# Eight of 24 modulation chunks multiplied on VectorE instead of TensorE

## The chip, the cores and the metric

One Trainium2 chip, one of its cores. The metric is the device time of one execution in microseconds; the kernel before was run three times (2601.99, 2604.31 and 2606.24 us, median 2604.31). One more execution was profiled, and all rows of the trace are from that one. [...]

## What is computed

Two blocks on 256 tokens of width 2048, in float32. The first block has an even and an odd attention layer and attends to a memory; the second has a recurrent (LRU) layer and a differential attention layer on the tokens and, in its first layer, on a context of 256 tokens. Every layer of the second block is modulated: shift, scale and gate come from a vector `c` (for the tokens) and a vector `c_ctx` (for the context), each multiplied with a matrix of 2048 x 6144.

```python
def second_block(x, c, ctx, c_ctx, mod_w, mod_b, ...):
    sc, scc = jax.nn.silu(c), jax.nn.silu(c_ctx)
    for i in range(DEPTH):                      # DEPTH = 2
        need_ctx_out = i < DEPTH - 1
        shift, scale, gate = jnp.split(sc @ mod_w[i] + mod_b[i], 3, axis=-1)
        cshift, cscale, cgate = jnp.split(scc @ mod_w[i] + mod_b[i], 3, axis=-1)
        h_lat = rms_norm_2(x, norm_g[i]) * (1.0 + scale[:, None]) + shift[:, None]
        h_ctx = rms_norm_2(ctx, norm_g[i]) * (1.0 + cscale) + cshift
        ...
        x = x + gate[:, None] * y_lat
        if need_ctx_out:
            ctx = ctx + cgate * y_ctx
```

The modulation needs nothing of the first block. Its two matrices are 100 MB of the kernel's 425 MB of loads. The gate of the context in the last layer (`cgate` for i = 1) is never used.

## The kernel before

**Weights.** All weights pass through a ring of 8 slots in SBUF (`ring`, RA). A unit of the ring is two k-tiles of 128 rows by 512 columns, 0.524 MB. SP issues one load for each unit, in the order of the list `RING`, and ahead of each it waits until TensorE has used the unit eight places before (`unit` in the sync program, `s_wused`). For a product in nearly full float32, ScalarE rounds each unit to `ring_hi` (`hi`, L1316; four buffers), VectorE subtracts that from the unit into `ring_lo` (`lo`, L1770), and TensorE does three products of each tile, hi x hi, hi x lo and lo x hi (`multiply`, L716): 12 matmuls a unit.

**Modulation.** The 24 chunks of 512 columns (12 for each of the two matrices, `MOD_CHUNK`) are "mod" units, 8 to a chunk, 192 in all. They aren't split; TensorE multiplies them as they landed, in float32, with the columns of `cond_t` (CS) as the stationary operand, 32 columns wide, into four groups of 32 partitions of PSUM bank 3 (`fill_mod`, L789). When a chunk is complete, VectorE copies the bank to SBUF (`mod_rows`, L1856), TensorE sums the four groups and turns rows to columns with `row_sums` (SEL) in four matmuls of two columns (`sum_mod`, L800), and VectorE adds the bias into `mod_t` (`mod_columns`, L1864). Where these two steps stand is set by `ROWS_BY` and `SUMS_BY`.

**Order.** The order of all work is written out by hand as lists of units. In the first block the heads of the attention layers are taken in turns of two. A turn has four gaps, filled with ring units so that TensorE multiplies while ScalarE and VectorE do the softmax (`Turn`, `lay_turns`, `head_turn`); `with_mod` puts pairs of mod units among them. There are 96 such pairs, from place 58 to 485 of the ring; in time they lie between 198 and 1093 us. In the odd layer a turn is, from its start, ring ring ring PAIR ring PAIR ring PAIR ring ring PAIR, with the scores after the first ring unit (L867), the transposes of the softmax (L879) after the second pair, and the products with the values (L894) two ring units and a pair later.

**Each engine follows the same list.** `follow` in the vector program takes a unit at a time: before anything that belongs to unit U it makes the lo parts up to `split_behind(U - 1)`, which is the smaller of four splits ahead and all splits up to place U + 4. ScalarE's `follow` does the same for the hi parts, after evicting a finished chunk from PSUM (L1391). After place 525 the program runs in loops (`s_modd` must have reached `N_MOD` by then).

Of the kernel before, what the change touches and what calls it, by code (L numbers as in the profile page):

```python
# [24 lines left out]
ALU = mybir.AluOpType  # L25
# [156 lines left out]
N_MOD = 24  # L182
MODS_OF_EVEN = 12
MOD_CHUNK = [(0, m) for m in range(10)] + [(1, 11)] + [(1, m) for m in range(11)] + [(0, 10), (0, 11)]
# [10 lines left out]
MOD_UNITS = iter(range(8 * N_MOD))  # L195


def with_mod(units, pairs):

    out, n = [], len(units)  # L200
    places = [-(-(j + 1) * n // (pairs + 1)) for j in range(pairs)]
    if (n, pairs) == (3, 2):
        places = [2, 3]
    for k in range(n + 1):
        for _ in range(places.count(k)):
            out += [("mod", next(MOD_UNITS)), ("mod", next(MOD_UNITS))]
        out += units[k:k + 1]
    return out
# [81 lines left out]
for _name, _u in RING:  # L290
    SPLIT_BEFORE.append(sum(_made))
    if _name == "mod":
        LO_BY.append(None)
        continue
    _pool = _name == "lru_in"
    LO_BY.append((_pool, _made[_pool]))
    _made[_pool] += 1
# [44 lines left out]
SUMS_BY[POS[OD_TURNS[-1].gaps[1][1]]] = N_MOD - 1  # L342
assert len(ROWS_BY) == len(SUMS_BY) == N_MOD and all(r <= s for r, s in zip(sorted(ROWS_BY), sorted(SUMS_BY)))

# [54 lines left out]
def build(nc, t, consts, out):  # L399
    ctx = ExitStack()  # L400
    with ctx:
# [11 lines left out]
        SEL = sb("row_sums", [P, 2])  # L413
# [80 lines left out]

        MODS_EV, MODS_OD = HB[:, TT * EV_W:TT * EV_W + CHUNK], a_qrt
# [62 lines left out]
        s_mods, s_modt, s_modd, s_msc = map(sem, ("mod_rows_ready", "mod_summed", "mod_ready", "mod_scale_ready"))  # L558
        s_dve = sem("vector_step")
# [42 lines left out]
        def _(sp):  # L602
# [12 lines left out]
            def unit(U, w, k0, nk, col, n, i=None, per=0):  # L615

                dst = raw(U, nk * n).rearrange("p (k n) -> p k n", k=nk)
                cols = col if i is None else sp.snap(col)

                if U + per >= SLOTS:  # L620
                    sp.wait_ge(*raw_free(U + per - SLOTS, i, per, 1 if per else 0))
                src = w.rearrange("(k p) n -> p k n", p=P)[:, k0:k0 + nk, bass.ds(cols, n)]
                sp.dma_start(dst, src).then_inc(s_w[U % SLOTS], 16)
# [9 lines left out]
            def weights(U, stage, u):  # L633

                c, j = divmod(u, units_of(stage))
                if stage == "mod":
                    layer, chunk = MOD_CHUNK[c]
# [62 lines left out]
        def _(pe):  # L700
# [4 lines left out]
            def multiply(U, k0, nk, kt, n, tiles, x, i=None, per=0, hold=None, order=None, tile_done=None):  # L705
# [13 lines left out]
                mm.then_inc(s_wused, 1)  # L719
# [60 lines left out]
            def fill_mod(u):  # L780
# [10 lines left out]
                mm.then_inc(s_wused, 1)  # L791

            def sum_mod(m, bank=MB):
# [5 lines left out]
                for j in range(4):  # L799
                    mm = pe.matmul(PS[:, bank, 2 * j:2 * j + 2], rows[:, j * P:(j + 1) * P], SEL[:], start=True, stop=True)  # L800
# [16 lines left out]
            def fill(units):  # L817
                for stage, u in units:
                    if POS[stage, u] in SUMS_BY:
                        sum_mod(SUMS_BY[POS[stage, u]])  # L820
                    if stage == "mod":
# [936 lines left out]
        def _(dve):  # L1758
# [99 lines left out]
            def mod_columns(m, bank=3):  # L1858

                dve.wait_ge(s_modt, m + 1)  # L1860
                layer, c = MOD_CHUNK[m]
                first = VEC_AT["mod_b_2"] + 48 * layer + 4 * c
                sums = PS[:, bank, 0:8].rearrange("p (k w) -> p k w", w=2)
                dve.tensor_tensor(out=MODT[:, layer, 4 * c:4 * c + 4, :], in0=sums, in1=GT[:, first:first + 4].unsqueeze(2).to_broadcast([P, 4, 2]),  # L1864
                                  op=ALU.add).then_inc(s_modd, 1)
# [27 lines left out]
            def follow(units):  # L1893

                for unit in units:
                    U = POS[unit]
                    lo_to(split_behind(U - 1))
                    ropes_behind(*unit)
                    if U in ROWS_BY:
                        mod_rows(ROWS_BY[U])  # L1900
# [77 lines left out]
            dve.tensor_reduce(SEL[:], ident.rearrange("p (g w) -> p w g", g=4)[:, 0:2, :], AX, ALU.add)  # L1978
# [63 lines left out]
            rstd(2, 4)  # L2042
            follow(EV_SECOND)
# [491 lines left out]
```

## Time and profile before

| | |
|---|---|
| median of 3 runs | 2604.31 us (2601.99 to 2606.24) |
| the profiled execution | 2607.06 us, span 2604.8 us |
| granted TensorE clock | 0.987 of full speed, mean |
| instructions | 31415, of them 12080 matmuls |
| loads | 421.45 MB read, 163 GB/s over the span |

The profile counts an engine as busy while an instruction of it runs; matmuls are pipelined, so their durations overlap and the step from one start to the next is what one costs. The slices are 40 equal parts of the span, 65.1 us each; a digit is a share in tenths, 9 being 90% or more. In a timeline a row is a group of like instructions (x8: eight), with its start and its length from the first start to the last end.

### The profile page before, as it was taken

What the parts mean: (1) busy time and instruction counts of PE and PEld (TensorE: products, weight loads), DVE (VectorE), ACT (ScalarE), POOL (GpSimd) and SP (SyncE); (2) the same over time, 40 slices, a digit from 0 to 9 for tenths busy, and PEclk for the clock granted to TensorE, in tenths of its full rate; (3) what the DMA queues carried; (4) which work ended last, traced back from release to release, by engine and by line L of the source; (5) the groups of instructions that cost most, each with busy time, mean ns of one, the idle gap of its engine ahead of it and who ended that gap; (6) DMA issues with size and microseconds to landing.
All of it is one profiled execution on the core that took longest, in us unless ns stands there. A gap on an engine that the chain in (4) does not pass through costs nothing.

```text
span 2604.8 us, 31415 instructions
## 1 busy us (share of the span) xinstructions
PE 2512.6 (96%) x12080; PEld 1960.3 (75%) x12080; DVE 1437.7 (55%) x1907; ACT 1171.0 (45%) x1719; POOL 228.8 (9%) x126
## 2 busy tenths in 40 slices
PE   6999999999999999999999999999799999999988
PEld 5887777777776677788777777787687877878767
DVE  4644444554545454566776767623545375654754
ACT  6444344553444334456555555422425344352542
POOL 0000000000000000002555553000000000000000
PEclk9999999999999999999999999999899999999989
DMA  6568777737787888864333332223234233342323
GB/s 217 178 186 270 244 239 252 239 98 233 241 270 258 285 283 272 287 220 138 102 94 94 90 93 92 98 97 97 81 97 137 82 121 103 91 131 87 121 81 129
DMA packets 275121, 425.22 MB, mean 163 GB/s; under 512 B 14374, under 2 KB 92988, under 8 KB 273852
## 3 DMA queue, kind: packets, MB, share of 16 engines
q1 hardware_dynamic: 273596, 418.09, 49.5%
q10 hardware_dynamic: 1408, 5.51, 0.5%
q8 instruction: 80, 1.31, 0.2%
q14 instruction: 37, 0.30, 0.0%
HBM read 421.45 MB, written 2.10 MB: 163 GB/s over the span
## 4 chain that ended last, share of the span: by engine, by line
PE 90%; ACT 4%; DVE 4%; issue 1%; DMA 1%; SPq 0%; ACTq 0%; DVEq 0%
PE ps L716 63%; PE ps L1097 13%; PE ps L789 3%; PE ps L1080 2%; ACT ring_hi L1316 1%; PE ps L867 1%; PE ps L894 1%; PE ps L1191 1%; PE ps L1209 1%; PE ps L767 1%; PE ps L1052 1%; DVE ring_lo L1770 1%; PE ps L800 1%; PE ps L879 1%; DMA ring<-in_od_w_in 0%
## 5 line engine op out<-in xcount | busy, mean ns | idle before, releaser
L1316 ACT CAST ring_hi<-ring 128x1024 fp32r<-128x1024 f32 (+2 forms) x590 | 610.9, 1038 | 1070.1 <-PE ps L716 620.5
L1770 DVE TENSOR_TENSOR ring_lo<-ring,ring_hi 128x1024 fp32r<-128x1024 f32 (+2 forms) x526 | 633.9, 1212 | 822.7 <-ACT ring_hi L1316 820.0
L716 PE MATMUL ps<-ring_hi,act_hi 128*128 128x512 f32 (+2 forms) x1272 | 513.2, 403 | 10.5 <-issue 4.4
L716 PE MATMUL ps<-ring_hi,act_lo 128*128 128x512 f32 (+2 forms) x1272 | 492.6, 387 | 0.0
L716 PE MATMUL ps<-ring_lo,act_hi 128*128 128x512 f32 (+2 forms) x1272 | 491.4, 386 | 0.0
L716 PE MATMUL ps<-ring_hi,features_hi 128*128 128x512 f32 x1152 | 462.9, 402 | 17.0 <-DVE features_lo L2205 7.4
L716 PE MATMUL ps<-ring_hi,features_lo 128*128 128x512 f32 x1152 | 453.3, 394 | 0.0
L716 PE MATMUL ps<-ring_lo,features_hi 128*128 128x512 f32 x1152 | 453.2, 393 | 0.0
L716 PEld LDWEIGHTS ps<-ring_hi,act_hi 128*128 128x128 f32 x1272 | 240.0, 189 | 112.8 <-issue 46.2
L716 PEld LDWEIGHTS ps<-ring_hi,features_hi 128*128 128x128 f32 x1152 | 219.1, 190 | 88.3 <-issue 32.2
L716 PEld LDWEIGHTS ps<-ring_hi,act_lo 128*128 128x128 f32 x1272 | 239.9, 189 | 50.9
L716 PEld LDWEIGHTS ps<-ring_lo,act_hi 128*128 128x128 f32 x1272 | 240.7, 189 | 42.4
L716 PEld LDWEIGHTS ps<-ring_hi,features_lo 128*128 128x128 f32 x1152 | 219.0, 190 | 47.4
L716 PEld LDWEIGHTS ps<-ring_lo,features_hi 128*128 128x128 f32 x1152 | 219.5, 191 | 43.1
L1097 PE MATMUL ps<-features_hi,ring_hi 128*128 128x512 f32 x480 | 192.8, 402 | 0.0
L1097 PE MATMUL ps<-features_lo,ring_hi 128*128 128x512 f32 x480 | 186.8, 389 | 0.0
L1097 PE MATMUL ps<-features_hi,ring_lo 128*128 128x512 f32 x480 | 186.8, 389 | 0.0
L2468 POOL TENSOR_TENSOR ring_lo<-ring,ring_hi 128x1024 fp32r<-128x1024 f32 x64 | 172.9, 2709 | 138.0 <-ACT ring_hi L1316 137.9
L1097 PEld LDWEIGHTS ps<-features_lo,ring_hi 128*128 128x128 f32 x480 | 90.1, 188 | 21.8 <-issue 3.6
L1097 PEld LDWEIGHTS ps<-features_hi,ring_hi 128*128 128x128 f32 x480 | 90.1, 188 | 21.8 <-issue 3.6
L1097 PEld LDWEIGHTS ps<-features_hi,ring_lo 128*128 128x128 f32 x480 | 90.1, 188 | 18.8
L789 PE MATMUL ps<-ring,cond_t 128*32 128x512 f32 x768 | 102.1, 604 | 0.0
(246 smaller groups left out, 2410.3 us busy)
## 6 DMA issues: line engine op xcount, KB each, us to landing
ring<-in_mod_w SPq DMA_DIRECT2D x192, 512.0 KB, 5.3
ring<-in_att_w_in SPq DMA_DIRECT2D x128, 512.0 KB, 3.6
ring<-in_ev_w_in SPq DMA_DIRECT2D x104, 512.0 KB, 4.9
ring<-in_od_w_in SPq DMA_DIRECT2D x96, 512.0 KB, 5.5
ring<-in_lru_w_in SPq DMA_DIRECT2D x64, 512.0 KB, 4.1
ring<-in_ev_w_out SPq DMA_DIRECT2D x40, 512.0 KB, 4.8
ring<-in_od_w_out SPq DMA_DIRECT2D x36, 512.0 KB, 4.8
ring<-in_lru_w_out SPq DMA_DIRECT2D x32, 512.0 KB, 3.6
```

What stands on the lines that cost most here:

```text
L716: mm = pe.matmul(PS[:, bank, 0:n], a, w[:, k - k0, :], start=(k == k_first and j == 0), stop=(k == k_last and j == 2))
L767: mm = pe.transpose(PS[:, 4 + q % 4, col:col + P], rows(tt, 2 * j + k), ident)
L789: mm = pe.matmul(PS[g:g + 32, MB, :], CS[:, 2 * k:2 * k + 32], raw(U)[:, k % 2 * CHUNK:(k % 2 + 1) * CHUNK], start=(k < 4), stop=(k >= KT ...
L800: mm = pe.matmul(PS[:, bank, 2 * j:2 * j + 2], rows[:, j * P:(j + 1) * P], SEL[:], start=True, stop=True)
L867: mm = pe.matmul(to, qt[:, tt * P:(tt + 1) * P], kt_[:, 0:n], start=True, stop=h is not MLA)
L879: mm = pe.transpose(PS[:, 4 + a, h.p_at(kt, tt):h.p_at(kt, tt) + P], S[:, a, s:s + P], ident)
L894: mm = pe.matmul(PS[:, 6 + a, tt * P:tt * P + w], PT[:, a, h.p_at(kt, tt):h.p_at(kt, tt) + P], rows, start=(kt == 0), stop=(kt == kts[-1]))
L1080: mm = pe.matmul(PS[:, 4 + j, :], GW[:, b, j, :], XC[:, b, :, :].rearrange("p c s -> p (c s)"), start=True, stop=True)
L1097: mm = pe.matmul(PS[:, part * 2 + b, :], W[:, w], x[:, kk, :], start=(kk == 0 and j == 0), stop=(kk == KT - 1 and j == 2))
L1316: act.copy(high(U, n), raw(U, n)).then_inc(s_hi, 1)
L1770: dve.tensor_tensor(out=low(U, n), in0=raw(U, n), in1=high(U, n).bitcast(F32), op=ALU.subtract).then_inc(s_lo, 1)
L2468: pool.tensor_tensor(out=low(U), in0=raw(U), in1=high(U).bitcast(F32), op=ALU.subtract).then_inc(s_lop, 1)
```

## The change

Eight of the 24 chunks become "vmod" units and keep 8 units each and their place in the ring's pattern: of the 96 pairs, 64 stay mod pairs and 32 become vmod pairs. `mod_stream` deals them out: 14 mod pairs first, then single vmod pairs among 4, 4, 3, 3, then 1, 2, 1 and 2 mod pairs. So four vmod pairs lie in the even layer, eight between places 231 and 307 (output of the even layer and the first chunks of the odd one), and twenty in the turns of the odd layer. The 16 chunks left to TensorE are the 12 of layer 0 and the first 4 of layer 1; VectorE gets the last 8 of layer 1.

For a vmod unit VectorE multiplies each k-tile, as it landed, by the column of `cond_t` that belongs to it, and adds this to an accumulator of 128 x 512 in SBUF (`mod_products`; VACC, in the buffer `mem_kv`, holds two chunks). Four of the chunks are made for both vectors, four (the last gate) for the tokens' vector alone. Every instruction waits for the last but one before it. The sum over the 128 partitions is done by TensorE, eight matmuls of one column a chunk, with a column of ones (SEL, now 3 columns wide) next to the sum of a mod chunk (`SUMMED_BESIDE`), and the bias is added beside that chunk's. TensorE skips vmod units; the ring unit ahead of them counts them as used (`VMODS_BEHIND`), and SP waits for VectorE's step count as well before it loads over one (`s_vmod`, `VMOD_STEPS`).

In the diff below context lines are cut to those next to a change.

```diff
@@ -179,9 +179,28 @@
 MEM_OD = Heads("mem_od", "plain", OD_QM, 0, MEMW, OD_GATE + OD_Y_M * P, OD_Y_M, None, SC128, mem=1)
-N_MOD = 24
-MODS_OF_EVEN = 12
-MOD_CHUNK = [(0, m) for m in range(10)] + [(1, 11)] + [(1, m) for m in range(11)] + [(0, 10), (0, 11)]
+N_MOD, N_VMOD = 16, 8
+MODS_OF_EVEN = 9
+MOD_CHUNK = [(0, m) for m in range(12)] + [(1, m) for m in range(12)]
+def wanted(m):
+    return 1 if MOD_CHUNK[m][0] == 1 and MOD_CHUNK[m][1] >= 8 else 2
+def mod_stream():
+    mine = [("mod", 2 * j) for j in range(4 * N_MOD)]
+    others = [("vmod", 2 * j) for j in range(4 * N_VMOD)]
+    out, mine = mine[:MODS_ALONE], mine[MODS_ALONE:]
+    for j, n in enumerate((4, 4, 3, 3) + 8 * (1,) + 4 * (2,) + 12 * (1,) + 4 * (2,)):
+        out += others[j:j + 1] + mine[:n]
+        mine = mine[n:]
+    assert not mine and len(out) == 4 * (N_MOD + N_VMOD)
+    return [(stage, u + j) for stage, u in out for j in range(2)]
@@ -192,7 +211,8 @@
-MOD_UNITS = iter(range(8 * N_MOD))
+MODS_ALONE = 14
+MOD_UNITS = iter(mod_stream())
@@ -203,7 +223,7 @@
         for _ in range(places.count(k)):
-            out += [("mod", next(MOD_UNITS)), ("mod", next(MOD_UNITS))]
+            out += [next(MOD_UNITS), next(MOD_UNITS)]
         out += units[k:k + 1]
@@ -289,7 +309,7 @@
     SPLIT_BEFORE.append(sum(_made))
-    if _name == "mod":
+    if _name in ("mod", "vmod"):
         LO_BY.append(None)
@@ -340,6 +360,17 @@
+SUMMED_BESIDE = {min((s, m) for s, m in SUMS_BY.items() if s > POS["vmod", 8 * p + 7])[1]: p for p in range(N_VMOD)}
+assert len(SUMMED_BESIDE) == N_VMOD
+VMOD_UNITS = [unit for unit in RING if unit[0] == "vmod"]
+VMOD_STEPS = dict(zip(VMOD_UNITS, np.cumsum([2 * wanted(N_MOD + u // 8) for _, u in VMOD_UNITS]).tolist()))
+VMODS_BEHIND = [0] * len(RING)
+for _at in range(len(RING) - 1):
+    while RING[_at + 1 + VMODS_BEHIND[_at]][0] == "vmod" and RING[_at][0] != "vmod":
+        VMODS_BEHIND[_at] += 1
+assert all(POS["vmod", 8 * p + 7] < s for s, m in SUMS_BY.items() if m in SUMMED_BESIDE for p in [SUMMED_BESIDE[m]])
+assert all(POS["vmod", 8 * p + 16] > s for s, m in SUMS_BY.items() if m in SUMMED_BESIDE for p in [SUMMED_BESIDE[m]] if p + 2 < N_VMOD)
 assert len(ROWS_BY) == len(SUMS_BY) == N_MOD and all(r <= s for r, s in zip(sorted(ROWS_BY), sorted(SUMS_BY)))
@@ -410,7 +441,7 @@
         CS = sb("cond_t", [P, 2 * KT + 32])
-        SEL = sb("row_sums", [P, 2])
+        SEL = sb("row_sums", [P, 3])
         MODT = sb("mod_t", [P, 2, 48, 2])
@@ -492,6 +523,7 @@
+        VACC = MKVB[:, 0:4 * CHUNK].rearrange("p (b w n) -> p b w n", b=2, w=2)
         MODS_EV, MODS_OD = HB[:, TT * EV_W:TT * EV_W + CHUNK], a_qrt
@@ -556,6 +588,7 @@
         s_mods, s_modt, s_modd, s_msc = map(sem, ("mod_rows_ready", "mod_summed", "mod_ready", "mod_scale_ready"))
+        s_vmod = sem("vector_mod_step")
         s_dve = sem("vector_step")
@@ -619,6 +652,8 @@
                     sp.wait_ge(*raw_free(U + per - SLOTS, i, per, 1 if per else 0))
+                    if i is None and RING[U - SLOTS] in VMOD_STEPS:
+                        sp.wait_ge(s_vmod, VMOD_STEPS[RING[U - SLOTS]])
                 src = w.rearrange("(k p) n -> p k n", p=P)[:, k0:k0 + nk, bass.ds(cols, n)]
@@ -633,8 +668,8 @@
                 c, j = divmod(u, units_of(stage))
-                if stage == "mod":
-                    layer, chunk = MOD_CHUNK[c]
+                if stage in ("mod", "vmod"):
+                    layer, chunk = MOD_CHUNK[c + (N_MOD if stage == "vmod" else 0)]
                     unit(U, t["mod_w_2"][layer], 2 * j, 2, chunk * CHUNK, CHUNK)
@@ -716,7 +751,7 @@
                         mm.then_inc(tile_done, 1)
-                mm.then_inc(s_wused, 1)
+                mm.then_inc(s_wused, 1 + (VMODS_BEHIND[U] if i is None else 0))
@@ -788,7 +823,7 @@
                                    start=(k < 4), stop=(k >= KT - 4))
-                mm.then_inc(s_wused, 1)
+                mm.then_inc(s_wused, 1 + VMODS_BEHIND[U])
@@ -797,7 +832,16 @@
                 for j in range(4):
-                    mm = pe.matmul(PS[:, bank, 2 * j:2 * j + 2], rows[:, j * P:(j + 1) * P], SEL[:], start=True, stop=True)
+                    mm = pe.matmul(PS[:, bank, 2 * j:2 * j + 2], rows[:, j * P:(j + 1) * P], SEL[:, 0:2], start=True, stop=True)
+                if m in SUMMED_BESIDE:
+                    p = SUMMED_BESIDE[m]
+                    pe.wait_ge(s_vmod, VMOD_STEPS["vmod", 8 * p + 7])
+                    both = wanted(N_MOD + p) == 2
+                    for j in range(4):
+                        for w in range(2):
+                            col = 8 + 2 * j + (w if both else 0)
+                            mm = pe.matmul(PS[:, bank, col:col + 1], VACC[:, p % 2, w, j * P:(j + 1) * P], SEL[:, 2:3],
+                                           start=both or w == 0, stop=both or w == 1)
                 mm.then_inc(s_modt, 1)
@@ -818,6 +862,8 @@
                         sum_mod(SUMS_BY[POS[stage, u]])
+                    if stage == "vmod":
+                        continue
                     if stage == "mod":
@@ -1858,11 +1904,34 @@
                 dve.wait_ge(s_modt, m + 1)
-                layer, c = MOD_CHUNK[m]
-                first = VEC_AT["mod_b_2"] + 48 * layer + 4 * c
-                sums = PS[:, bank, 0:8].rearrange("p (k w) -> p k w", w=2)
-                dve.tensor_tensor(out=MODT[:, layer, 4 * c:4 * c + 4, :], in0=sums, in1=GT[:, first:first + 4].unsqueeze(2).to_broadcast([P, 4, 2]),
-                                  op=ALU.add).then_inc(s_modd, 1)
+                for chunk, at_ in ([(N_MOD + SUMMED_BESIDE[m], 8)] if m in SUMMED_BESIDE else []) + [(m, 0)]:
+                    layer, c = MOD_CHUNK[chunk]
+                    n = wanted(chunk)
+                    first = VEC_AT["mod_b_2"] + 48 * layer + 4 * c
+                    sums = PS[:, bank, at_:at_ + 8].rearrange("p (k w) -> p k w", w=2)[:, :, 0:n]
+                    ins = dve.tensor_tensor(out=MODT[:, layer, 4 * c:4 * c + 4, 0:n], in0=sums,
+                                            in1=GT[:, first:first + 4].unsqueeze(2).to_broadcast([P, 4, n]), op=ALU.add)
+                ins.then_inc(s_modd, 1)
+            def mod_products(unit):
+                p, j = divmod(unit[1], 8)
+                U, n = POS[unit], wanted(N_MOD + p)
+                done = VMOD_STEPS[unit] - 2 * n
+                if j == 0 and p >= 2:
+                    dve.wait_ge(s_modt, {q: m for m, q in SUMMED_BESIDE.items()}[p - 2] + 1)
+                dve.wait_ge(s_w[U % SLOTS], landed(U))
+                for k in range(2 * j, 2 * j + 2):
+                    rows = raw(U)[:, k % 2 * CHUNK:(k % 2 + 1) * CHUNK]
+                    for w in range(n):
+                        acc, by = VACC[:, p % 2, w if n == 2 else k % 2, :], CS[:, 2 * k + w:2 * k + w + 1]
+                        if j == 0 and (k == 0 or n == 1):
+                            ins = dve.tensor_scalar(acc, rows, by, None, ALU.mult)
+                        else:
+                            dve.wait_ge(s_vmod, done - 1)
+                            ins = dve.scalar_tensor_tensor(out=acc, in0=rows, scalar=by, in1=acc, op0=ALU.mult, op1=ALU.add)
+                        ins.then_inc(s_vmod, 1)
+                        done += 1
@@ -1896,6 +1965,8 @@
                     ropes_behind(*unit)
+                    if unit in VMOD_STEPS:
+                        mod_products(unit)
                     if U in ROWS_BY:
@@ -1975,7 +2046,8 @@
             dve.wait_ge(s_const, 16)
-            dve.tensor_reduce(SEL[:], ident.rearrange("p (g w) -> p w g", g=4)[:, 0:2, :], AX, ALU.add)
+            dve.tensor_reduce(SEL[:, 0:2], ident.rearrange("p (g w) -> p w g", g=4)[:, 0:2, :], AX, ALU.add)
+            dve.memset(SEL[:, 2:3], 1.0)
             dve.wait_ge(s_vec, 4)
@@ -2040,6 +2112,7 @@
             rstd(2, 4)
+            dve.wait_ge(s_cs, 1)
             follow(EV_SECOND)
```

## Rows read from the trace of the kernel before

**Rows 1.** The page: TensorE's busy line, then TensorE and DMA in 40 slices.

```profile
PE 2512.6 (96%) x12080; PEld 1960.3 (75%) x12080; DVE 1437.7 (55%) x1907; ACT 1171.0 (45%) x1719; POOL 228.8 (9%) x126
...
PE   6999999999999999999999999999799999999988
...
DMA  6568777737787888864333332223234233342323
```

**Rows 2.** Busy time by engine in two stretches, granted clock, DMA share, GB/s.

```profile
200.00:700.00 500.00, 494.45 (x2495) 372.61 (x2494) 245.97 (x346) 218.44 (x313) 0.00 (x0) 1.00 0.69 227
700.00:1110.00 410.00, 407.78 (x2241) 291.81 (x2240) 207.24 (x401) 177.01 (x292) 2.00 (x4) 1.00 0.81 273
```

**Rows 3.** The same columns, two slices of 10 us in the odd layer.

```profile
990.00:1000.00 10.00, 10.00 (x60) 6.99 (x59) 3.92 (x5) 3.54 (x4) 0.00 (x0) 1.00 0.98 340
...
1010.00:1020.00 10.00, 10.00 (x56) 6.49 (x54) 2.88 (x5) 2.31 (x7) 0.00 (x0) 1.00 0.58 185
```

**Rows 4.** Waits, 700 to 1110 us: total us, times, longest.

```profile
ACT ring_hi L1316 <- DMA ring<-in_od_w_in: 165.3, 71, 8.5
...
PEld ps L716 <- DVE ring_lo L1770: 10.5, 12, 1.3
```

**Rows 5.** The matmuls of line L789: ns min/median/max, first and last start.

```profile
L789 PE MATMUL ps<-ring,cond_t x768: 592/593/617, 198.1 to 1093.3; 128*32 128x512 f32 x192
```

**Rows 6.** Timeline of TensorE around a mod pair: start us, us, the instruction.

```profile
881.44 0.39 PE L716 MATMUL ps<-ring_hi,act_lo 128*128 128x512 f32 x1
881.76 1.07 PE L789 MATMUL ps<-ring,cond_t 128*32 128x512 f32 x8
882.76 0.50 PE L716 MATMUL ps<-ring_hi,act_hi 128*128 128x512 f32 x1
```

**Rows 7.** Timeline of TensorE around a sum over partitions.

```profile
1011.04 0.39 PE L716 MATMUL ps<-ring_hi,act_lo 128*128 128x512 f32 x1
1011.27 0.95 PE L800 MATMUL ps<-row_sums,arena 128*128 128x2 f32 x8
1012.08 0.49 PE L716 MATMUL ps<-ring_hi,act_hi 128*128 128x512 f32 x1
```

**Rows 8.** Timeline of SP in one turn; landing times, 760 to 1100 us.

```profile
869.68 4.04 SPq L623 DMA_DIRECT2D ring<-in_mod_w  x2
874.34 0.88 SPq L623 DMA_DIRECT2D ring<-in_od_w_in  x2
...
DMA to landing us min/median/max: 3.4/5.6/7.5
```

**Rows 9.** Timeline of ScalarE in that turn, with what ended its idle time.

```profile
880.04 1.05 ACT L1316 CAST ring_hi<-ring 128x1024 fp32r<-128x1024 f32 x1 [5.06 <-DMA ring<-in_od_w_in]
881.35 1.05 ACT L1316 CAST ring_hi<-ring 128x1024 fp32r<-128x1024 f32 x1 [0.25 <-DMA ring<-in_od_w_in]
```

**Rows 10.** Timeline of VectorE in that turn: the lo parts.

```profile
869.74 1.22 DVE L1770 TENSOR_TENSOR ring_lo<-ring,ring_hi 128x1024 fp32r<-128x1024 f32 x1
...
875.01 1.23 DVE L1770 TENSOR_TENSOR ring_lo<-ring,ring_hi 128x1024 fp32r<-128x1024 f32 x1 [3.98 <-ACT ring_hi L1316]
881.13 1.22 DVE L1770 TENSOR_TENSOR ring_lo<-ring,ring_hi 128x1024 fp32r<-128x1024 f32 x1 [4.89 <-ACT ring_hi L1316]
...
883.20 1.22 DVE L1770 TENSOR_TENSOR ring_lo<-ring,ring_hi 128x1024 fp32r<-128x1024 f32 x1
```

**Rows 11.** Timeline of TensorE in that turn: the pair in question, the later unit.

```profile
873.25 1.06 PE L789 MATMUL ps<-ring,cond_t 128*32 128x512 f32 x8
...
886.87 0.48 PE L716 MATMUL ps<-ring_hi,act_hi 128*128 128x512 f32 x1
```

**Rows 12.** Two VectorE multiply-adds: all of one line; three chained in a timeline.

```profile
L2315 DVE SCALAR_TENSOR_TENSOR second_block<-second_block,head_stats x32: 750/751/755, 1988.5 to 2525.3; 128x512 f32<-128x512 f32 x32
...
1312.10 2.32 DVE L2170 SCALAR_TENSOR_TENSOR second_block<-ps,scalars,second_block 128x508 f32<-128x508 f32 x3
```

## Prediction

> **What bounds the kernel now.** I read the page first: TensorE is busy 96% of the span and at 9 tenths in nearly every slice, while the DMA row is high only in the first 18 slices, where the modulation weights go through the ring [rows 1]. The table of stretches narrows this down. From 200 to 1110 us TensorE is busy 902 of 910 us at the full clock, VectorE 453 us, GpSimd 2 us; the DMA share is 0.69 up to 700 us and 0.81 after it [rows 2]. So work taken off TensorE there shortens the span one for one, as long as VectorE and the ring follow. The 10 us slices show how near the ring is to its limit: one moves 340 GB/s at a share of 0.98, the next but one 185 at 0.58 [rows 3]; at 340 GB/s a ring unit of 0.524 MB takes 1.54 us. Third, the waits: in the odd layer (700 to 1110 us) ScalarE waits 165 us in 71 places for od_w_in to land [rows 4]. That wait is mostly covered, but it says that hi and lo parts are made as soon as weights land, not from stock. Fourth, the timelines of one turn in which I follow the ring [rows 8 to 11].
>
> **What leaves TensorE.** 192 mod units make 768 records, four each [rows 5]. A pair of units stands between ring units: the last matmul before it starts at 881.44, the first behind it at 882.76; less the usual step of 0.23 us that is 1.09 us a pair [rows 6]. 64 units, 32 pairs, leave: -34.8 us. If only part of that step were freed the saving would be lower, but both neighbours are ordinary ring units that elsewhere follow each other at 0.23 us, so I take all of it.
>
> **What comes to TensorE.** Before, a sum over partitions (four f32 matmuls, eight records) is 24 times there; the one at 1011.27 takes 1012.08 - 1011.04 - 0.23 = 0.81 us [rows 7]. After, 16 remain, and 8 of them get eight more matmuls of one column: 16 x 0.81 + 8 x 1.62 = 25.9 against 19.4 us, so +6.5 us. Two columns or one hardly matter, since eight weight loads with 128 columns each are the same; I bound it at 5 and 9 us. Each of the 8 also waits for VectorE's last product; it comes 8 to 44 ring positions behind that product, eight of them being some 17 us of TensorE's time, so I put this at nothing.
>
> **What comes to VectorE.** Four chunks for two vectors (4 x 16 x 2) and four for one (4 x 16): 192 instructions on 128x512, 8 of them plain products for n=2 and 8 for n=1. The nearest row is the multiply-add from SBUF with a pointer scalar, 751 ns; three such that wait for each other take 2.32 us [rows 12]. Here each waits for the last but one, so successive ones can overlap their ends: I take 0.67 us, between 0.60 and 0.78. A two-vector unit costs 2.7 us, a one-vector unit 1.35 us; in sum 129 us (115 to 150), less 8 copies of rows (-5). VectorE then has some 577 of 880 us: it does not become the bound by its sum. As cover, what VectorE does there is mostly waiting for ring_hi (3.98 and 4.89 us in one turn) [rows 10]. The extra small additions to mod_t and SEL cost under 2 us and are covered likewise.
>
> The Trainium skill (VectorE: DVE Perf Modes, The DRAIN you can't avoid) says that the next operation starts only once the pipe is empty, and that a semaphore after each costs nothing extra. The chain of three above agrees with a full duration and a little more per step; by that rule a unit would take 3.0 or 1.5 us and the VectorE sum 144 us, and the forecast would move up by some 2 us.
>
> **What the ring pays.** This is the disputed term. A mod unit gives its slot back when TensorE has passed it, 0.54 us each. A vmod unit gives it back when VectorE has multiplied it, and in VectorE's program that stands behind the lo parts of units up to four positions ahead; SP waits in order, so every later issue is queued behind it. I follow the pair in places 362 and 363 of the ring (vmod 32 and 33, one vector) in the turn from 862 us.
> Before: TensorE reaches it at 873.25; SP issues the two units that take their slots, od_b 34 and 35, at 874.34 and 874.8; they land 5.7 and 6.5 us later (ScalarE starts at 880.04 and 881.35); their lo parts end at 882.35 and 884.4; TensorE starts od_b 34 at 882.76, 0.4 us behind its lo part, and od_b 35 at 886.87, 2.4 us behind it [rows 6, 8 to 11].
> After: the lo part before the first ends at 870.96, so its products end at about 872.3, ahead of TensorE. SP then issues od_b 34 at 873.8, once the place in front is free; with 5.7 us to land, 1.05 for hi and 1.2 for lo it is ready at 881.7. TensorE comes to it 2 x 1.09 us earlier than before (this pair, and vmod 34 and 35, which stood at 881.76), at 880.6: 1.1 us late. The second unit's products stand behind the lo part that ends at 876.24 and end at 877.6, so its slot is issued at 877.8, 3 us later than before; ready at about 885.7 to 886.6. TensorE, already late by 1.1, wants it at 885.8: 0 to 0.8 us more. So a turn that saves 2.18 us gives 1.1 to 1.9 back; I take 1.3, the nearer end, since later issues meet an emptier queue.
> Eight such turns: +10.4 us. For the four two-vector pairs of the first turns (vmod 24 to 31) the second product ends 1.35 us later still, but only every second or third pair has left TensorE: 1.1 to 2.6, taken as 1.5 each, +6. For the eight pairs between 611 and 763 us there are more ring units between pairs and no table of scores in the way: 0 to 1.6, taken as 0.5 each, +4. For the four before 480 us: 0, the DMA share is 0.69 there. All together +20.4. About 4 us of the added sums fall into places where TensorE now waits anyway, so -4.
> What VectorE owes TensorE in a head's turn (copies of p, the gate products) comes after a product of at most 2 x 2.7 us; VectorE itself waits for TensorE in front of them, so I add nothing, with 0 to 3 us as bounds.
>
> **Sum.** -34.8 + 6.5 + 20.4 - 4 = -11.9 us. The profiled execution took 2607.06 us (span 2604.8), 0.1% over the median of 2604.31; taking the change off the median gives 2592.4.
>
> **Rivals.**
> 1. The whole gain comes through (2576). If units that are issued later land in 3.4 us, the least seen, instead of 5.6 [rows 8], od_b 34 is ready at 879.4 and od_b 35 at 883.6, both before TensorE: no stalls, -34.8 + 6.5 = -28.3. For it: the landing time is long when several transfers run at once. Against: the share only rises, from 0.81 to about 0.87. The Trainium skill (DMA: Bandwidth & Descriptors, Anatomy of one DMA) gives 2.0 us and the bytes at 436 GB/s, which would be 3.2 us for a unit alone; by it this rival would hold. The trace agrees for the least value only.
> 2. In the odd layer the stream of weights sets the time (2600). Then the 20 pairs there bring nothing, and 12 x 1.09 - 6.5 = 6.6 remain, less 2 to 4 for the eight middle pairs: -4. For it: slices at a share of 0.98 [rows 3]. Against: a turn of 28.1 us has 15 units, 23.1 us at full rate, which fits in 25.9.
> 3. Slots come back too late, and the kernel is slower (2613). The cycle is: lo part, products, issue, landing, hi, lo. It has two landings between TensorE leaving one unit and wanting the one behind the pair. If the second landing is 7 us (the most seen is 7.5) rather than 5.7, a turn loses 2.6 instead of 1.3 and saves 2.18: +3.4 over eight turns; the two-vector pairs lose 2.3 against 1.09 (+4.8), the middle ones 0.9 against 1.09 (-1.5), the first four save 4.4, the sums cost 6.5: about +9. It decides from a mean loss of 0.9 us a pair over all 32 (28.3 / 32). For it: TensorE already reaches such a unit 0.4 us behind its lo part once a turn. Against: the first unit of a pair is mostly freed earlier than before.
> That the work does not leave TensorE can't be: the pairs are simply not in its program.
>
> **How the numbers follow.** A measurement of this kernel can tell a change from none down to about 0.2%, 5.2 us. Forecast 2592.4: 0.45, of which a tenth within 0.2%. Rival 1: 0.15. Rival 2: 0.20, at its edge, so a third of it faster, the rest the same. Rival 3: 0.20, with some of it the same. Faster 0.62, same 0.19, slower 0.19. The range takes rival 1 but for its last 2 us and rival 3 up to 2612: 2578 to 2612.
>
> **What would show it.** TensorE's records of L789's line fall from 768 to 512, and the mean step over a sum of both kinds is 1.6 us. VectorE's products take 0.67 us start to start, and its busy time rises by 120 to 130 us. In the turns ring_lo releases TensorE more often: its waits for ring_lo, 10.9 us from 700 to 1110 us before, go to 25 to 30. If they stay under 12, rival 1 holds; if the DMA share in the turns is over 0.95, rival 2; if SP waits long for vector_mod_step and TensorE's waits are over 40 us, rival 3. The prediction is wrong at its root if the time before 600 us changes by more than the 4.4 us saved there.

## The result: 2613.95 us, slower by 0.38%

Seven runs of the changed kernel gave a median of 2613.95 us (2612.3 to 2616.47) against 2604.31 for the kernel before (seven runs as well, 2601.99 to 2606.69); the ratio is 1.0038, with a 95% interval of 1.0027 to 1.0050. The forecast was 2592.4, with a range up to 2612: the sign was wrong and the time lies outside the range. It is almost the time of the third rival (2613), but by luck: that rival's sum holds 37 us of waits for late slots and nothing for the clock; the trace has 28.7 us of waits of all kinds, and 8.9 us of low clock.

The page after, for [rows 1]: TensorE's and VectorE's busy lines, then the granted clock and the DMA in 40 slices.

```profile
PE 2499.0 (96%) x11888; PEld 1975.3 (76%) x11888; DVE 1555.0 (59%) x2092; ACT 1170.8 (45%) x1719; POOL 230.7 (9%) x126
...
PEclk9999999999999999999999999999899999999989
DMA  5558777637677887764333332223234233342323
```

TensorE is busy 14 us less and VectorE 117 us more, and the span is 9.1 us longer. What gave the time back shows in the two stretches of [rows 2], with the columns PE, PEld, DVE, ACT, POOL, clock, DMA share, GB/s:

```profile
200.00:700.00 500.00, 490.95 (x2456) 377.63 (x2455) 291.17 (x417) 220.97 (x316) 0.00 (x0) 1.00 0.68 230
700.00:1110.00 410.00, 386.67 (x2032) 291.04 (x2031) 272.66 (x502) 168.46 (x282) 3.00 (x4) 0.97 0.78 266
```

From 700 us on TensorE is idle 23.3 us where it had been idle 2.2 us, and its granted clock is 0.97 where it had been 1.00. The DMA share from 700 us on fell from 0.81 to 0.78. To see where each microsecond went I set the start of every ring unit on TensorE beside the start of the same unit before:

| ring places | 32 pairs gone | sums | low clock | waits, rest | sum |
|---|---|---|---|---|---|
| 122 to 229 (even layer) | -4.4 | -1.6 | 0 | -0.3 | -6.3 |
| 230 to 315 | -8.7 | +1.7 | +1.4 | +7.0 | +1.4 |
| 316 to 360 (first turns, two vectors) | -4.4 | +0.8 | +2.3 | +7.8 | +6.5 |
| 361 to 488 (turns, one vector) | -17.4 | +5.8 | +5.2 | +14.2 | +7.8 |
| all | -34.9 | +6.7 | +8.9 | +28.7 | +9.4 |

The first column is 1.09 us a pair; the second 0.81 us for a plain sum and 1.64 more for one over VectorE's accumulators (negative where plain sums have gone elsewhere); the third adds up what steps of wide matmuls at 0.43 us have over 0.23; the fourth is the rest. The idle time of TensorE in the trace grows by 24.6 us from 200 to 1110 us (32.4 where it had been 7.8) and carries most of the fourth column, so that column holds waits of every kind. The third column counts wide matmuls alone and is, for that, rather too small.

**The low clock.** A sum after, on TensorE, for [rows 7]:

```profile
873.80 0.95 PE L835 MATMUL ps<-row_sums,arena 128*128 128x2 f32 x8
874.61 1.93 PE L843 MATMUL ps<-row_sums,mem_kv 128*128 128x1 f32 x16
876.39 0.49 PE L751 MATMUL ps<-ring_hi,act_hi 128*128 128x512 f32 x1
...
877.62 0.63 PE L751 MATMUL ps<-ring_lo,act_hi 128*128 128x512 f32 x1
878.05 0.63 PE L751 MATMUL ps<-ring_hi,act_lo 128*128 128x512 f32 x1
```

The 16 records of one column take 1.78 us. TensorE isn't idle for a moment, yet from 877.2 on the wide matmuls last 0.63 us and follow each other at 0.43 instead of 0.23 us. The table of stretches has the granted clock there:

```profile
877.00:880.00 3.00, 3.00 (x9) 2.36 (x8) 2.00 (x5) 1.05 (x1) 0.00 (x0) 0.53 0.47 180
```

0.53, the mean of these 3 us, is the lower level, 1.2 GHz, for all but the first moment. It lasts until 880.6 and costs 1.55 us. Of the eight falls from 600 to 1110 us, five come within 2 us behind a sum of this kind; the other three (832.8, 1034.2 and 1061.5 us) come within 1.4 us behind a wait of TensorE of 1.8 to 3.8 us.

**The waits.** Who held up TensorE's matmuls from 200 to 1110 us (total us, times, longest). In the kernel before, all its waits there were 7.8 us together, 0.4 of them for ring_lo and none for mod_t:

```profile
PE ps L751 <- DVE ring_lo L1816: 9.2, 11, 1.7
PE ps L824 <- DVE mod_t L1912: 6.3, 3, 3.8
PE ps L751 <- ACT proj L1437: 4.6, 3, 2.0
PE ps L913 <- ACT arena L1458: 3.8, 2, 2.0
PE ps L940 <- DVE arena L2016: 3.6, 4, 1.2
```

The second I had not priced at all. VectorE and TensorE around the longest of them:

```profile
821.64 0.69 DVE L1902 COPY arena<-ps 128x512 f32<-128x512 f32 x1
822.24 5.39 DVE L1932 SCALAR_TENSOR_TENSOR mem_kv<-ring,cond_t,mem_kv 128x512 f32<-128x512 f32 x8
827.53 1.23 DVE L1816 TENSOR_TENSOR ring_lo<-ring,ring_hi 128x1024 fp32r<-128x1024 f32 x1
...
830.24 1.22 DVE L1816 TENSOR_TENSOR ring_lo<-ring,ring_hi 128x1024 fp32r<-128x1024 f32 x1
831.37 0.16 DVE L1912 TENSOR_TENSOR mod_t<-ps,vectors_t 128x8 f32<-128x8 f32 x1
```

```profile
827.35 0.39 PE L751 MATMUL ps<-ring_hi,act_lo 128*128 128x512 f32 x1
831.58 1.07 PE L824 MATMUL ps<-ring,cond_t 128*32 128x512 f32 x8 [3.84 <-DVE mod_t L1912]
833.34 0.63 PE L751 MATMUL ps<-ring_lo,act_hi 128*128 128x512 f32 x1
```

Eight products of a two-vector pair run in a row for 5.39 us. Behind them stand a lo part, the gate products, another lo part, and only then the addition of 0.16 us that frees bank 3 for the next mod unit. TensorE waits 3.84 us for it, and the matmuls after this wait run at the lower clock too.

The waits for ScalarE (L1437, which takes a finished chunk out of PSUM, and L1458, which copies q and k for the scores) have their causes further back. Ahead of the longest of the first kind ScalarE had waited for VectorE; ahead of both of the second kind it had waited for a load (one of the two is shown):

```profile
839.88 0.40 ACT L1467 ACTIVATE arena<-arena,head_stats 128x128 f32<-128x128 f32 x1 [4.59 <-DVE head_stats L2007]
...
1031.67 1.04 ACT L1362 CAST ring_hi<-ring 128x1024 fp32r<-128x1024 f32 x1 [5.08 <-DMA ring<-in_od_w_in]
1032.63 1.07 ACT L1458 COPY arena<-ps 128x512 f32<-128x512 f32 x2
```

**SP** (SyncE, which issues the loads) now waits for VectorE as well: 142 us in 55 places from 200 to 1110 us. All its waits together hardly changed (728 us, 722 before), so the 142 us are a sign of who frees a slot last, and no measure of how late loads are.

```profile
SPq L658 <- PE ps L751: 543.0, 206, 7.4
SPq L656 <- DVE mem_kv L1932: 141.9, 55, 7.1
SPq L658 <- PE ps L824: 43.2, 59, 3.6
```

### The profile page after: what moved, and what is told of

Read it like the earlier page. It is cut to its first block, busy times and chain, and to the rows that moved or that the text cites. A ratio compares the mean times of both kernels' runs of the same rounds, so it can differ in the third digit from the quotient of the medians.

```text
span 2613.9 us, 31326 instructions
## 1 busy us (share of the span) xinstructions
PE 2499.0 (96%) x11888; PEld 1975.3 (76%) x11888; DVE 1555.0 (59%) x2092; ACT 1170.8 (45%) x1719; POOL 230.7 (9%) x126
## 4 chain that ended last, share of the span: by engine, by line
PE 84%; DVE 5%; ACT 4%; DMA 4%; issue 2%; SPq 1%; ACTq 0%; DVEq 0%
PE ps L751 58%; PE ps L1143 12%; DMA ring<-in_od_w_in 3%; PE ps L1126 2%; PE ps L824 2%; ACT ring_hi L1362 2%; DVE ring_lo L1816 1%; PE ps L913 1%; PE ps L802 1%; PE ps L1237 1%; DVE mem_kv L1932 1%; PE ps L1255 1%; PE ps L940 1%; PE ps L1098 1%; PE ps L843 1%
## 5 line engine op out<-in xcount | busy, mean ns | idle before, releaser
L1932 DVE SCALAR_TENSOR_TENSOR mem_kv<-ring,cond_t,mem_kv 128x512 f32<-128x512 f32 x176 | 120.3, 747 | 0.0
```

The costliest lines, as they stand in the source:

```text
L1932: ins = dve.scalar_tensor_tensor(out=acc, in0=rows, scalar=by, in1=acc, op0=ALU.mult, op1=ALU.add)
```

## Experiments

Each is compared with runs of the kernel before on the same chip; its ratio to that, with a 95% interval, is given. The changed kernel's is 1.0038.

**Two ends: VectorE's part and TensorE's part taken away.**

x1 drops TensorE's extra matmuls (the loops around these two lines go with them):

```diff
-                            mm = pe.matmul(PS[:, bank, col:col + 1], VACC[:, p % 2, w, j * P:(j + 1) * P], SEL[:, 2:3],
-                                           start=both or w == 0, stop=both or w == 1)
```

> The changed kernel without the eight extra matmuls of each of the eight sums over VectorE's accumulators (their part of the modulation is left out of the result; TensorE still waits for VectorE's last product). Theory: the sums cost 1.64 us each on the path (16 records of one column, 1.78 us in the trace, less the usual start gap) and each is followed by some 3.4 us at the 1.2 GHz level of TensorE's clock, worth up to 1.6 us. Taking them away gives back 8 x 1.64 = 13 us and 8 to 10 us of clock: 2614 goes to about 2592, and the granted clock from 700 to 1100 us returns to 0.99 or more. Rival A: the clock falls because of the waits for VectorE and the ring, not because of the sums; then only 13 us come back (2601) and the clock stays near 0.97. Rival B: the time in the turns is set by the ring, and freed TensorE time turns into waits: less than 5 us come back (2609 or more).

2595.4 us, 0.9970 (0.9958 to 0.9981): 18.6 us under the changed kernel. The clock from 700 to 1110 us is back at 0.99, so rivals A and B fall. TensorE's waits for mod_t rose from 6.3 to 11.5 us, so a part of the saving was turned into waits.

x2 shortens VectorE's products (one instruction a unit stands for all two or four):

```diff
-                            ins = dve.scalar_tensor_tensor(out=acc, in0=rows, scalar=by, in1=acc, op0=ALU.mult, op1=ALU.add)
+                dve.tensor_scalar(VACC[:, p % 2, 0, 0:2], raw(U)[:, 0:2], CS[:, 4 * j:4 * j + 1], None, ALU.mult).then_inc(s_vmod, 2 * n)
```

> The changed kernel with one two-column product for each vmod unit in the place of its two or four products of 512 columns (their part of the modulation is wrong then); the place in VectorE's program where the slot is given back is kept. Theory: VectorE's own time makes most of TensorE's extra waits (24 us more than before): the time falls by 15 to 20 us, to 2594 to 2599, with the sums and their clock still paid. Rival: it is the place of the release, behind the lo parts of later units, that makes the ring late, not the length of the products: then the time falls by less than 5 us and the waits for ring_lo stay at 20 us or more.

2589.1 us, 0.9941 (0.9925 to 0.9958): 24.8 us under the changed kernel, more than was expected. TensorE's waits in 700 to 1110 us go from 23.3 to 10.7 us, SP's for VectorE from 142 to 41 us, while the order of everything is the same. So it is the length of the products and not merely their place. The clock stays at 0.98, since the long sums are still there.

x4 leaves out both, and SP's wait for VectorE with them:

```diff
+                if i is None and U >= SLOTS and RING[U - SLOTS] in VMOD_STEPS:
+                    sp.wait_ge(s_w[U % SLOTS], landed(U - SLOTS))
...
-                        sp.wait_ge(s_vmod, VMOD_STEPS[RING[U - SLOTS]])
...
-                        mod_products(unit)
```

> The changed kernel without VectorE's products, without the eight extra sums, and with SP waiting only for the unit ahead (and for the slot's own landing) before it loads over a vmod unit; that part of the modulation is left out. It is the floor of this change: 32 pairs gone from TensorE and nothing in their place. Theory: 32 x 1.09 = 35 us under the kernel before, 2569. Rival: the stream of weights sets the time in the odd layer, whose 20 pairs then bring nothing: 2590, with a DMA share over 0.9 there.

2566.7 us, 0.9862 (0.9845 to 0.9878): 37.2 us under the kernel before. 32 pairs and the 8 plain sums that are gone too make 34.9 + 6.5 = 41.4, so 4 us of it did not reach the end. Its two stretches:

```profile
200.00:700.00 500.00, 495.03 (x2473) 380.42 (x2472) 251.14 (x354) 227.09 (x324) 0.00 (x0) 1.00 0.71 233
700.00:1110.00 410.00, 401.25 (x2117) 304.62 (x2116) 219.29 (x410) 188.17 (x303) 4.53 (x6) 1.00 0.84 288
```

The loads went from 273 to 288 GB/s and TensorE was still busy 401 of 410 us: the stream of weights did not set the time, so the prediction's second rival falls. From this floor the products alone cost 28.6 us (x1) and the sums alone 22.4 (x2); together 47.2 (the changed kernel). That is 3.8 less than their sum, about what the prediction had let the sums absorb, but it is within the scatter of the runs. x2 still has SP's wait for VectorE, and x1 TensorE's, so neither is quite one part alone.

**The sums alone, with no work on VectorE.** x5 is the kernel before with

```diff
+                if m in (7, 9, 11, 14, 16, 18, 20, 23):
+                    for j in range(4):
+                        for w in range(2):
+                            mm = pe.matmul(PS[:, bank, 8 + 2 * j + w:9 + 2 * j + w], rows[:, j * P:(j + 1) * P], SEL[:, w:w + 1], start=True, stop=True)
```

> The kernel before with eight extra one-column matmuls (16 records) behind eight of its 24 sums, at nearly the places where the changed kernel has its sums; nothing else is changed, and VectorE does nothing more. Theory: 8 x 1.64 = 13 us of matmuls and 8 to 12 us of low clock: 2625 to 2630, with the clock at 1.2 GHz for some 3 us after most of them. Rival: narrow matmuls alone don't lower the clock; then 2617 and the granted clock stays at 1.00. By the prediction on record (0.81 us each) it would be 2611.

2625.3 us, 1.0081 (1.0064 to 1.0098): +21.3 us, of which 14.2 are the matmuls (8 x 1.78, or 13.1 as a step) and the rest is clock. One of the eight:

```profile
698.19 0.95 PE L800 MATMUL ps<-row_sums,proj 128*128 128x2 f32 x8
699.00 1.93 PE L804 MATMUL ps<-row_sums,proj 128*128 128x1 f32 x16
700.78 0.49 PE L716 MATMUL ps<-ring_hi,act_hi 128*128 128x512 f32 x1
...
702.20 0.63 PE L716 MATMUL ps<-ring_lo,act_hi 128*128 128x512 f32 x1
...
704.75 0.39 PE L716 MATMUL ps<-ring_lo,act_hi 128*128 128x512 f32 x1
```

No wait, no VectorE work, and the same fall of the clock. (The 2611 in the expectation takes half of what the prediction's own working gives: it had counted the eight matmuls of a sum at 1.62 us, which gives 2617.)

**The same sums, but not in a row.** x6 puts the accumulators' matmuls a ring unit ahead of the mod sum:

```diff
+VSUMS_BY = {SPLIT_UNITS[SPLIT_UNITS.index(s) - 1]: m for s, m in SUMS_BY.items() if m in SUMMED_BESIDE}
...
+                    if POS[stage, u] in VSUMS_BY:
+                        sum_vmod(VSUMS_BY[POS[stage, u]])
```

> The changed kernel with the eight matmuls over VectorE's accumulators moved one ring unit ahead of the sum of the mod chunk, so that 16 and 8 narrow records (1.8 and 0.8 us) stand apart by 12 wide matmuls instead of 24 in a row (2.6 us). Work and result are the same. Theory: it is the length of the stretch of narrow matmuls that brings the clock to its lower level; apart, it falls less often or not at all, and 5 to 10 us come back: 2604 to 2609. Rival: 1.8 us of them are already enough; then the clock falls as often as before and the time stays at 2612 to 2616.

2609.2 us, 1.0021 (1.0010 to 1.0032), some 4 us under the changed kernel, but the two intervals overlap (the changed kernel's begins at 1.0027), so the gain isn't clear of noise. The trace is clearer than the time. By the granted clock, stretches of 24 narrow records (one or two columns) in a row, 2.6 us, were followed by the lower clock (it falls in their last 0.8 us or within 2 us behind them) in 5 of 8 cases in the changed kernel, 5 of 8 in x5, 5 of 8 in x2 and 7 of 8 in x7: 22 of 32, in most of them for 1.5 to 1.7 us of extra time in the wide matmuls behind. None of the 8 stretches of 16 records in x6 brought it down. One ran at the lower clock from its start, which had come 0.9 us earlier, behind a wait of 3.0 us for ScalarE. Of the 24 stretches of 8 records in the kernel before none was followed by it. The time gained little because the traced run still has 27.3 us at the lower clock from 200 to 1110 us (24.6 in the changed kernel), now always beside a wait of TensorE of 2.0 to 3.8 us.

**The order on VectorE.** x7 puts the products first:

```diff
+                    if unit in VMOD_STEPS:
+                        mod_products(unit)
                     lo_to(split_behind(U - 1))
                     ropes_behind(*unit)
-                    if unit in VMOD_STEPS:
-                        mod_products(unit)
```

> The changed kernel with VectorE's products of a vmod unit ahead of the lo parts that stood in front of them, so that the slot comes back earlier and the lo parts come later by 1.35 or 2.7 us. Theory: the 25 us that the products cost are VectorE's lateness in all that it owes TensorE (lo parts, bias additions, copies of the softmax), so the order matters little: 2609 to 2620. Rival (the prediction's stall term): late slots make the loads late; then earlier slots bring 8 to 15 us, 2599 to 2606, and SP's waits for the accumulators fall well under 142 us.

2603.3 us, 1.0001 (0.9990 to 1.0011): 10 us under the changed kernel. My theory missed and the rival held: slots that come back late do cost, and SP's waits for VectorE fell from 142 to 98 us. The lo parts, now later, did not hold TensorE up more (7.3 against 9.2 us). So of the 25 us that the length of the products costs, about 10 hang on where they stand. Late slots are the likely way, but the edit also lets products run while VectorE would wait for ring_hi, and the two were not told apart. The rest lies, as far as the trace goes, in VectorE's own lateness (mod_t 5.1 us here, copies and scores) and in the clock. How it divides between them was not tried.

**Place and amount.** x8 leaves TensorE all chunks but the four for one vector, and deals their 16 pairs out early:

```diff
-N_MOD, N_VMOD = 16, 8
+N_MOD, N_VMOD = 20, 4
...
-    for j, n in enumerate((4, 4, 3, 3) + 8 * (1,) + 4 * (2,) + 12 * (1,) + 4 * (2,)):
+    for j, n in enumerate(7 * (1,) + (3,) + 7 * (1,) + (49,)):
```

> Only the four chunks for one vector go to VectorE (16 pairs), all between places 122 and 307 of the ring, that is in the even layer and up to the first chunks of the odd one; the turns of the odd layer are as in the kernel before. Theory: every pair brings its 1.09 us there (-17.4), four sums cost 1.64 each and their clock (+6.6 +4), waits 0 to 3: about -5, 2599. Rival: the even layer's turns lose to VectorE as the odd ones did, and it is no faster than before.

2592.3 us, 0.9962 (0.9948 to 0.9977): 10 to 11 us under the kernel before, twice the gain that was expected. From 200 to 1110 us TensorE is idle 5.9 us, less than the 7.8 of the kernel before: these pairs cost it no waits. x9 adds VectorE's two accumulators of a chunk and halves the sum:

```diff
+                if add:
+                    dve.wait_ge(s_vmod, done)
+                    acc = VACC[:, p % 2, 0, :]
+                    dve.tensor_tensor(out=acc, in0=acc, in1=VACC[:, p % 2, 1, :], op=ALU.add).then_inc(s_vmod, 1)
```

> The same with VectorE adding its two accumulators of a chunk at the end (one more instruction of 0.7 us), so that a sum takes four matmuls of one column instead of eight: 16 narrow records in a row (1.6 us) instead of 24. Theory: 4 x 0.8 us of matmuls less, and the clock stays up: -17.4 + 3.3 + 0 to 3, 2590 to 2593. Rival: 1.6 us of narrow matmuls lower the clock too; then 2595 to 2597.

2585.0 us, 0.9933 (0.9916 to 0.9950), 5 us less than the lower end of what was expected. None of its four stretches of 16 narrow records is followed by the lower clock; of the four of 24 in x8, two are. x13 is the same work in the turns (`MODS_ALONE = 48`, one pair in two from place 317 to 429):

> The same work as in the early one-vector kernel with the added halves (four one-vector chunks, 16 pairs, four matmuls a sum; 2585), but dealt out between places 317 and 429, one pair in two, in the turns of the odd layer. Theory: what VectorE's products cost depends on the place: in the turns late slots and late lo parts give back about half of the 17 us, so 2591 to 2597. Rival: only the two-vector pairs and the long sums cost; then the place makes no difference and it is within 3 us of 2585.

2594.2 us, 0.9965 (0.9950 to 0.9981). The same 16 pairs bring 18 us early and 9 to 11 us in the turns, where TensorE is idle 13.0 us from 200 to 1110 us instead of 6.9 and SP waits 57 us for VectorE instead of 42. x11 is x9 with the products first:

> The early one-vector kernel with added halves, and VectorE's products ahead of the lo parts. Theory: early on the slots are not what is late (SP waits 42 us in all for the accumulators, against 142 in the changed kernel), so the order brings 0 to 3 us: 2582 to 2585. Rival: it brings its share of the 10 us that it brought in the changed kernel, 5 us or more: under 2580.

2582.4 us, 0.9915 (0.9898 to 0.9931): 22 us under the kernel before and the fastest version that does the whole work. x12 has all eight chunks where the change puts them, with the three edits together:

> All eight chunks on VectorE as in the changed kernel, with the three edits together: products ahead of the lo parts, halves added on VectorE for the one-vector chunks, and the sums over accumulators one ring unit ahead of the mod sum. Theory: the edits add up: 2603 (products first) less 3.3 (matmuls) less 6 (clock): 2593 to 2596. Rival: the time freed on TensorE in the turns goes into waits for VectorE: 2599 or more.

2595.9 us, 0.9960 (0.9945 to 0.9974). As expected, the edits add up, and the change as it was planned gains some 10 us once its sums and its order are mended. None of its stretches of 16 narrow records is followed by the lower clock either. x14 took six chunks:

> Six chunks on VectorE (two for two vectors first, then the four for one), eight pairs in the even layer, eight up to place 307, and eight spread over the turns, one in five pairs; products first, halves added, sums apart. Theory: 24 x 1.09 = 26 us less 2 x 1.64 + 4 x 0.81 = 6.5 and 0 to 6 of waits: 2583 to 2590, no better than the four early chunks (2585). Rival: waits stay small where pairs are spread: 2580 or less.

2639.0 us, 1.0130 (1.0101 to 1.0158), some 50 us or more off both expectations. VectorE's copy of bank 3 and the sum that reads it fell on the same ring unit for five chunks (places 334 to 445) and on neighbours for a sixth (370 and 371), and TensorE waits for the copy each time. The accumulators' sum at place 461 adds a seventh wait, of 6.4 us:

```profile
PE ps L837 <- DVE arena L1910: 31.8, 6, 6.9
```

The kernel before has such a place too (129), where TensorE waits 1.9 us. The run says nothing on six chunks, but shows what a wait costs when both ends of it are put at one place of the list.

## Why the prediction was wrong

The error is 21.3 us: the table adds up to +9.4 where -11.9 was said. Of it the low clock, which the sum doesn't have, makes 8.9; the waits make 12.3 (28.7 where 20.4 - 4 was said); the matmuls of the sums 0.2.

- **What bounds the kernel**: right. In x4 37 of the 41 us that left TensorE reached the end, and the ring could bring it.
- **What leaves TensorE**: right. The start of the next ring unit moved by 1.08 to 1.23 us a pair, 1.09 was said.
- **What comes to TensorE**: the matmuls right, +6.6 where +6.5 was said; what follows them was missing, and this is one of the two steps that failed. It took the sum as more of a row of 8 records, but 24 in a row is a thing that the trace of before doesn't show. The lower clock behind them and behind waits cost 8.9 us and had been put at nothing without a word; x5 shows it with no work on VectorE. It should have been a term with a bound from below of 0 and, had every sum lost 1.6 us, from above of 13.
- **What comes to VectorE**: the price right (5.39 us for eight, 0.67 each; 117 us more busy, a little under the 120 to 130 said).
- **What the ring pays**: the mechanism right, and by the prediction's own sign the size nearly so. TensorE's waits for ring_lo from 700 to 1110 us, those of its weight loads and of its matmuls, were to go from 10.9 to 25 to 30 us; they went to 23.0:

```profile
PEld ps L751 <- DVE ring_lo L1816: 15.2, 13, 2.1
...
PE ps L751 <- DVE ring_lo L1816: 7.8, 9, 1.7
```

  By stretches all waits were 7.0 against 4 from place 230 to 315, 7.8 against 6 in the two-vector turns, 14.2 against 10.4 in the one-vector ones, but these hold VectorE's debts too. In the turn that the prediction followed, the two loads were issued at 874.46 and 878.93 (873.8 and 877.8 said) and landed after 4.5 us; the lo parts ended at 881.26 and 885.73. Yet TensorE, which was to come at 880.6, came to od_b 34 only at 885.37 and didn't wait: a sum over accumulators (1.64) and the low clock behind it (1.57) stood ahead of it. So the loss of 1.3 us that was taken for each of these turns is not seen in the very turn from which it was worked out.
- **What VectorE owes TensorE**: this is the other step that failed. It was put at nothing, with 3 us as its bound, because VectorE waited for TensorE in front of these steps before. Waits for mod_t alone are 6.3 us. The additions to mod_t had been looked at as work (0.16 us) and not as a link: bank 3 is free only after it, it stands behind the products in VectorE's list, and the next mod unit stands right behind the sum in TensorE's. A wait of 2.0 us at 844.5 leads back through ScalarE to VectorE as well. The copies of p make 3.6 us (0.4 before), but ahead of two of these four waits VectorE itself had waited 5 and 6 us for ring_hi; these, and the scores' 3.8 us through ScalarE, belong rather to late loads. An exact share for each can't be read from the runs: x7 puts about 10 us on the place of the products and x2 25 us on their length.
- **Rivals**: the landing time did not shorten (5.5 us median, 5.6 before), so the first falls, and with it the estimate of 3.2 us from the formula of the Trainium skill (DMA: Bandwidth & Descriptors, Anatomy of one DMA) as a guide to this ring; the page gives that formula for loads that GpSimd issues, and here SP does. Nor was it a floor: the least was 2.7 us. The second falls by x4. The third gave the time but not by its cause: it needed 37 us of waits for slots (2.6, 2.3 and 0.9 us for its three kinds of places) and TensorE's waits over 40 us, and they were 32.4 us of all kinds.
- **The Trainium skill on VectorE** (VectorE: DVE Perf Modes, The DRAIN you can't avoid) says that the next operation starts only once the pipe is empty; the same paragraph adds that one that isn't held starts earlier. The trace bears out the second where each instruction waits for the last but one: they last 747 ns and follow each other at 0.67 us. The chain of three in [rows 12] takes 0.77 us each.
- **The range**: it ended 2 us short. The unknown terms (clock, links through VectorE) had been set to nothing instead of bounded.

## What to carry to other kernels

Work moved to an engine with half of its time free still stands in a list there: go through everything that stands behind it in that list, and for each find who waits, however short the instruction is. Small matmuls in a row have a price that their own time doesn't show (here 24 records, not 16); put them apart, or let another engine make them fewer. Moving work pays first where the engine's timeline has slack and buffers come back early (here the even layer), so deal it out by place and not evenly.

## What the runs showed of the hardware

TensorE's clock fell to 1.2 GHz with TensorE busy throughout: after 24 records of one or two columns in 2.6 us, in 22 of 32 cases (changed kernel, x2, x5 and x7) and in 2 of 4 in x8, mostly for 1.5 to 1.7 us of extra time. Of the 24 stretches of 16 such records that began at the full clock (x6, x9, x11, x12, x13, x14) none was followed by it. I had thought of it only in connection with idle time. The Trainium skill (TensorE: Matmul & The Clock Gate, Part 1: The HAM clock gate) speaks of idle and busy; by these traces a stretch of narrow matmuls in which the engine is never idle can be followed by the lower level as idle time is.
